# Taking 128 of 512 tokens out of a dense expert product and summing their gathered rows on VectorE

## What is computed

```
q = (hf @ w_q).reshape(T, 8, 2, 128)
s = einsum("thpd,hpkd->thpk", q, sub_keys)          # 128 keys per half
... top 16 per half, top 16 of their 256 sums per head
idx  = i1 * 128 + i2                                # 8 heads x 16 = 128 experts per token, of 16384
gate = softmax(best_v)
a    = einsum("tmd,td->tm", u_tab[idx], x)          # up: one dot product per picked expert
wgt  = gate * gelu(a)
y    = einsum("tm,tmd->td", wgt, v_tab[idx])        # down: weighted sum of the picked value rows
```

## Time and profile before

| | |
|---|---|
| median of 3 runs | 3601.62 us (3600.2 to 3602.76) |
| profiled execution, its own time | 3602.71 us |
| its span, first to last instruction | 3600.7 us |
| TensorE, VectorE, ScalarE, GpSimd busy | 97%, 67%, 29%, 12% |
| up stage of layer 0, gate chunks | about 605 to 1022 us |
| down stage, layer 0 | about 1109 to 1815 us |
| DMA traffic | 633.62 MB, mean 176 GB/s |

### The profile page before, as it was taken

How to read it: one execution, slowest core, us unless ns; L and a number is a source line. 1 busy time by engine, 2 the same in 40 slices (tenths; PEclk the granted TensorE clock), 3 DMA queues, 4 the chain that set the end, 5 groups by cost and what they waited for, 6 DMA issues and landing times.

```text
span 3600.7 us, 56122 instructions
## 1 busy us (share of the span) xinstructions
PE 3503.5 (97%) x16668; PEld 2836.9 (79%) x16668; DVE 2422.0 (67%) x6622; ACT 1039.3 (29%) x1382; POOL 438.8 (12%) x186
## 2 busy tenths in 40 slices
PE   5999999999999999999999999999999999999998
PEld 3578888888887888888875788888888888888886
DVE  6973996999924666665577159969999055555555
ACT  3333223444432212121242332234444312121122
POOL 0033443000031000000001334410000400000000
PEclk8999999999999999999999999999999999999999
DMA  6152443555547777786621224435555566666663
GB/s 221 58 215 90 146 143 138 186 199 216 216 181 222 243 235 243 243 244 195 181 93 37 78 97 143 146 132 216 216 181 204 204 204 193 193 192 195 190 196 119
DMA packets 442868, 633.62 MB, mean 176 GB/s; under 512 B 285984, under 2 KB 286368, under 8 KB 440352
## 3 DMA queue, kind: packets, MB, share of 16 engines
q1 hardware_dynamic: 402752, 495.60, 43.5%
q10 hardware_dynamic: 40032, 137.07, 9.7%
HBM read 496.26 MB, written 136.31 MB: 176 GB/s over the span
## 4 chain that ended last, share of the span: by engine, by line
PE 78%; DVE 16%; issue 3%; DMA 1%; ACT 1%; DVEq 0%; SPq 0%; ACTq 0%
PE bank L563 26%; PE bank L439 22%; PE bank L567 13%; PE bank L443 11%; PE bank L546 3%; DVE z_pad L1095 2%; DVE h L1060 2%; DVE h L1063 2%; DVE h L1062 1%; DVE h L1059 1%; DVE scratch L969 1%; DVE z_pad L1093 1%; DVE h L1096 1%; DVE u_pad L1061 1%; PE bank L362 1%
## 5 line engine op out<-in xcount | busy, mean ns | idle before, releaser
L598 ACT ACTIVATE w_hi<-ring 128x1024 fp32r<-128x1024 f32 x584 | 618.9, 1060 | 2243.0 <-PE bank L567 1110.7
L439 PE MATMUL bank<-h_hi,w_hi 128*128 128x512 f32 x2528 | 1000.3, 396 | 5.1 <-ACT scratch L598 2.3
L439 PE MATMUL bank<-h_lo,w_hi 128*128 128x512 f32 x2528 | 985.8, 390 | 0.0
L563 PE MATMUL bank<-v_hi,w_hi 128*128 128x512 f32 x2032 | 792.1, 390 | 5.7 <-DVE v_lo L1146 5.7
L563 PE MATMUL bank<-v_lo,w_hi 128*128 128x512 f32 x2032 | 791.8, 390 | 0.0
L782 POOL TENSOR_TENSOR w_lo<-ring,w_hi 128x1024 fp32r<-128x1024 f32 x172 | 437.1, 2543 | 1717.1 <-ACT w_hi L598 1717.1
L443 PE MATMUL bank<-h_hi,w_lo 128*128 128x512 f32 x2528 | 624.2, 389 | 0.0
L439 PEld LDWEIGHTS bank<-h_hi,w_hi 128*128 128x128 f32 x2528 | 474.8, 188 | 105.1 <-ACT w_hi L598 4.9
L443 PEld LDWEIGHTS bank<-h_hi,w_lo 128*128 128x128 f32 x2528 | 474.5, 188 | 98.5
L439 PEld LDWEIGHTS bank<-h_lo,w_hi 128*128 128x128 f32 x2528 | 474.9, 188 | 97.2 <-issue 1.4
L1131 DVE TENSOR_SCALAR h<-iota_b,keys 128x128 f16<-128x128 f16 x2048 | 543.5, 308 | 0.0
(11 more groups left out here) (147 smaller groups left out, 1990.9 us busy)
## 6 DMA issues: line engine op xcount, KB each, us to landing
ring<-u_t SPq DMA_DIRECT2D x256, 512.0 KB, 3.3
ring<-v_t SPq DMA_DIRECT2D x256, 512.0 KB, 3.4
ga_scratch<-norm_tmp ACTq DMA_DIRECT2D x256, 256.0 KB, 2.0
g_scratch<-scratch ACTq DMA_DIRECT2D x16, 4096.0 KB, 13.4
scratch<-ga_scratch SPq DMA_DIRECT2D x256, 256.0 KB, 3.8
scratch<-g_scratch SPq DMA_DIRECT2D x256, 256.0 KB, 4.2
scratch<-ada_t SPq DMA_DIRECT2D x76, 512.0 KB, 5.3
ring<-wq_t SPq DMA_DIRECT2D x32, 512.0 KB, 3.4
```

The source lines that it names most:

```text
L439: pe.matmul(to, w_hi[:, b, k * P:(k + 1) * P], part_h[:, k, :], start=(k == 0 and part_h is h_hi), stop=False)
L563: pe.matmul(bank[:, k, :], w_hi[:, b, k * P:(k + 1) * P], part_w[:, b, :], start=(first and part_w is v_hi), stop=False)
L598: return act.activation(to, of, ACT.Copy)
```

## The change

The last 128 tokens (`OWN` = 128) leave the gate matrix and the down product, which keep `TD` = 384 tokens. Those 128 tokens have 128 picks each. For each pick number there is one gather of a value row per token (128 rows of 4 KB), and VectorE adds it, times its weight, to `own_y` (tokens on the partitions). Their up product stays dense. The GELU values that belong to their picks are gathered from `ga_dram` one value at a time, 128 gathers of 128 values.

The parts of the diff that matter:

```
+    OWN = 128
+    TD = T - OWN
+    PICKS = HEADS * TOPK
+    TURNS = PICKS // PER_ROW
+    ROWS = 3
+    TOK = 8
+    EARLY, LATE = RETRIEVING + 2 * RING, TD // TOK
+    ADDS = 2 * ROWS
+    ADD_FIRST = 10
+    ADD_LAST = ADD_FIRST + TURNS // ADDS
+    ADA_AT = 1
```

SyncE, `load_back`: gates by pairs of chunks, 384 tokens; four chunks are loaded ahead, not three:

```
+                    if n % 2:
+                        pair = n // 2 % 2
+                        sp.dma_start(g_in[:, pair, :, :], g_dram[:, :, bass.ds(RING * first + (n - 1), 2), :]
+                                     .rearrange("b p c t -> p b (c t)")).then_inc(g_landed[pair], 16)
+                    sp.dma_start(ga_in[:, slot, :], ga_dram[c][:, 0:TD]).then_inc(ga_landed[slot], 16)
-                for n in range(RING - 1):
+                for n in range(RING):
                     load_back(0, n)
```

TensorE:

```
-                            pe.matmul(bank[:, k, :], w_hi[:, b, k * P:(k + 1) * P], part_w[:, b, :],
+                            pe.matmul(bank[:, k, 0:TD], w_hi[:, b, k * P:(k + 1) * P], part_w[:, b, 0:TD],
...
+                pe.wait_ge(own_done, l + 1)
...
+                    pe.matmul(bank[:, k, TD:T], own_y[:, k * P:(k + 1) * P], fold[:, :], start=True, stop=True)\
+                      .then_inc(down_done, 1)
```

ScalarE:

```
+                act.wait_ge(own_ready, l + 1)
+                for half in range(PER_ROW):
+                    for own, of in zip((own_i, own_e, own_g), picked):
+                        act.dma_start(own[half * OWN:(half + 1) * OWN, :], of[P - OWN:P, half * TURNS:(half + 1) * TURNS])\
+                           .then_inc(own_spread, 16)
...
+                def split_v(r, n):
+                    b = n % 2
+                    act.wait_ge(w_step, N_V * l + RING * r + (n + 1))
+                    wait_product(act, l, r, stages["v"] + n - 2)
+                    copy(v_hi[:, b, 0:TD], ga_in[:, n % RING, :]).then_inc(v_high, 1)
```

GpSimd (the low halves of the last up chunks go to VectorE):

```
+                pool.wait_ge(own_spread, 48 * PER_ROW * (l + 1))
+                def fetch_rows(n):
+                    pool.wait_ge(rows_used, TURNS * l + n + 1)
+                    pool.indirect_dma_start(own_rows[n % ROWS], None, v_rows,
+                                            bass.IndirectOffsetOnAxis(ap=own_i[:, n:n + 1].bitcast(U32), axis=0))\
+                        .then_inc(rows_landed[n % ROWS], 16)
+                for n in range(ROWS):
+                    fetch_rows(n)
+                for s in range(RING):
+                    pool.wait_ge(ga_stored[s], 16 * (N_U // RING) * l + 16 * (N_U // RING) + 16)
+                for n in range(TURNS):
+                    pool.indirect_dma_start(own_w[:, n:n + 1], None, ga_cells,
+                                            bass.IndirectOffsetOnAxis(ap=own_e[:, n:n + 1].bitcast(U32), axis=0))\
+                        .then_inc(cells_landed, 16)
+                for n in range(ROWS, TURNS):
+                    fetch_rows(n)
```

VectorE:

```
+                def add(n, i):
+                    s = i % ROWS
+                    dve.wait_ge(rows_landed[s], 16 * (TURNS // ROWS + (s < TURNS % ROWS)) * l + 16 * (ADDS // ROWS) * n
+                                + (16 * (i // ROWS) + 16))
+                    dve.wait_ge(rows_used, TURNS * l + ADDS * n + (ROWS + i))
+                    dve.scalar_tensor_tensor(own_y, own_rows[s], own_w[:, bass.ds(ADDS * n + i, 1)], own_y,
+                                             ALU.mult, ALU.add).then_inc(rows_used, 1)
...
+                def step(r, s, with_ada, own, last=False):
+                    low_halves(r, s)
+                    if not last:
+                        weights(r, s + 1)
+                    if own:
+                        own(r, s)
+                    if with_ada and s < ADA_STEP:
+                        wait_ada(dve, ada_landed, 16, l, s, r - ADA_AT)
+                        modulate(s, ADA_STEP * (r - ADA_AT) + s)
...
+                def late_add(r, s):
+                    for i in range(ADDS * s // RING, ADDS * (s + 1) // RING):
+                        add(r - ADD_FIRST, i)
+                def some_rounds(with_ada):
+                    rounds(ADA_AT, ADD_FIRST, with_ada, None)
+                    dve.wait_ge(cells_landed, 16 * TURNS * l + 16 * TURNS)
+                    dve.tensor_tensor(own_w, own_w, own_g, ALU.mult).then_inc(own_weighed, 1)
+                    dve.wait_ge(own_weighed, 2 * l + 2)
+                    settle(dve)
+                    rounds(ADD_FIRST, ADA_AT + ADA_ROUNDS, with_ada, late_add)
```

More of the change, by code:

```diff
@@ L117, in hybrid_encoder @@
         coef = sb("coef", [P, 2, KC])
+        fold = ident
+        row_base = sb("row_base", [P, 1])
+        own_token = sb("own_token", [P, 1])
         def part(at, n):
@@ L1150, in weights @@
                        .then_inc(tile_used[s], 1)
-                def rounds(start, end, with_ada):
+                def step(r, s, with_ada, own, last=False):
[7 more added lines that the diff above has]
+                        modulate(s, ADA_STEP * (r - ADA_AT) + s)
@@ L1153, in rounds @@
+                def rounds(start, end, with_ada, own):
                     with dve.Fori(start, end) as r:
                         for s in range(RING):
-                            weights(r, s)
-                            if with_ada and s < ADA_STEP:
-                                wait_ada(dve, ada_landed, 16, l, s, r)
-                                modulate(s, ADA_STEP * r + s)
+                            step(r, s, with_ada, own)
+                def late_add(r, s):
+                    for i in range(ADDS * s // RING, ADDS * (s + 1) // RING):
+                        add(r - ADD_FIRST, i)
@@ new lines, in some_rounds @@
+                def some_rounds(with_ada):
[5 more added lines that the diff above has]
+                    rounds(ADD_FIRST, ADA_AT + ADA_ROUNDS, with_ada, late_add)
+                weights(0, 0)
+                rounds(0, ADA_AT, False, None)
@@ L1160, in _ @@
                 with dve.If(l < LAST):
-                    rounds(0, ADA_ROUNDS, True)
+                    some_rounds(True)
                 with dve.Else():
-                    rounds(0, ADA_ROUNDS, False)
-                rounds(ADA_ROUNDS, N_V // RING, False)
+                    some_rounds(False)
+                rounds(ADA_AT + ADA_ROUNDS, ADD_LAST, False, late_add)
+                for i in range(REST):
+                    add(TURNS // ADDS + 0 * l, i)
+                dve.wait_ge(rows_used, TURNS * l + TURNS + ROWS)
@@ L1165, in _ @@
+                dve.nop().then_inc(own_done, 1)
+                assert ADD_LAST == N_V // RING - 1
+                for s in range(RING):
+                    step(N_V // RING - 1, s, False, None, s == RING - 1)
                 for k in range(KC):
```

164 lines of the change are left out of this document (102 added, 62 removed).

## The result

The changed kernel takes 3714.2 us (median of 4 runs, 3710.0 to 3719.3), the kernel before 3602.2 on the same chip: ratio 1.0317, with a 95% interval of 1.0304 to 1.033. It is 3.2% slower, where 3416 us and 5% faster were forecast. 298 us are missing, and they lie in one place.

The account below looks back on a forecast made before the run. TensorE, busy 97% of the span, was taken to bound the kernel. 3602.7 -327.7 (down product) -32.2 (gate stage) -2.9 (seam) +3.8 (folds) +166 (transfers) +8 (cells) -1.1 (median) gave 3416 us, range 3310 to 3560.

Parts of the forecast that it names:

- the cells: Down stage before round 10: 128 gathers of single values a layer end slightly late, +4 us a layer, +8 us.
- Down product, 173.3 ns: Down product: 384 columns instead of 512 make each matmul 173.3 ns and a chunk 4.16 us, 327.7 us less.
- Rival (d): Down product: weight loads bind at 188 ns, +32 us, 3448 us in all; chance 0.08, counted inside the main 0.52.
- Gate stage: Up product: 48 chunks instead of 64 carry gates, 32.2 us less over 2 layers.
- seam: Between up and down product: 8.1 us go, 2.6 us without cover are new, twice; net 2.9 us less.
- folds: End of the down stage: eight fold products of 128 columns in full f32 a layer, +3.8 us.
- VectorE: Down stage: VectorE alone would add 21 us in 15 of layer 0's rounds; no separate term in the sum.
- Transfers in the rounds with adds: Down stage, rounds 10 to 30: transfers stretch chunks to 5.6 and 4.9 us, +104 and +62, together +166 us.
- the prediction's lower bound of 4.4 us: Rounds 10 to 30: a chunk's transfers without modulation take 4.4 us at full rate, over the 4.16 us beat.
- A gather costs GpSimd 1.3 us: Down stage: each of the 128 cell gathers a layer was taken to cost GpSimd 1.3 us.
- Rival (c): Cells in the down stage: gathers above 2.02 us make the kernel slower than before; 3724 us at 2.5; chance 0.13.
- Nothing added for the port: Down stage: VectorE's two-input operations beside GpSimd's gathers were taken not to slow down, so 0 us added.

Follow-up runs that it names:

- e11: The changed kernel without the gathers of cells and value rows and without the 256 adds on VectorE; 3249.5 us.
- e3: The changed kernel with all 128 gathers of 4-byte pieces reading the same 128 neighbouring values; 3448.3 us.
- e12: The changed kernel with a wait before each cell gather for a value that is long reached, so nothing is paced; 3667.9 us.
- e14: The changed kernel with the first cell gather waiting until the down product has come to chunk 10; 3687.2 us.
- v2: The changed kernel, whole computation, 4-byte gathers paced at 2.7 a chunk, the last 32 behind row fetches, weighed in two parts; 3425.9 us.
- e16: As e10, but cell gather n waits for chunk n*39/128; 3493.3 us.
- e10: The changed kernel with cell gather n waiting until the down product has come to chunk n*40/128; 3447.0 us.
- e9: The changed kernel with the 128 cell gathers replaced by plain GpSimd copies of 4-byte pieces 256 KB apart; 3399.6 us.
- e7: The changed kernel with indexed 4-byte gathers where partition p always reads the first value of chunk p, 256 KB from the next; 3711.9 us.
- v1: The changed kernel, whole computation, gathering pieces of 256 bytes from which VectorE takes the own token's value with a mask; 3428.8 us.
- e15: The changed kernel with the cell gathers in bursts of 16, each waiting until the one before has landed; 3570.7 us.
- e13: The changed kernel with one small GpSimd write before each of the 128 cell gathers; 3659.6 us.
- e4: The changed kernel with the cell gathers replaced by 128 plain GpSimd copies of 4-byte pieces out of one chunk, 2 KB apart; 3401.7 us.

## Why the prediction was wrong

The step that failed is the last term of the sum, "the cells": "+4 us a layer, +8". It asked what 128 gathers cost GpSimd and whether they would be done in time. It didn't ask what they do to TensorE while they run.

1. *Down product, 173.3 ns.* Right: 1101.21 to 1101.38, and 24 of them from 1101.21 to 1105.37, 4.16 us. Rival (d) is out; the loads follow at the same distance though each is written with 188 ns.
2. *Gate stage, seam, folds, VectorE.* Right in sum: e11 has none of the terms behind them and takes 3249.5 for 3243. The seam itself was forecast too short. TensorE waits 3.59 us there (3.58 in layer 1) and not 2.6, and the stretch at the 1.2 GHz level is still there, with starts 0.32 us apart from 1096.71 to 1099.59, some 1.5 us lost, where nothing was put down for it. Together that is 2.5 us a layer, most of the 6.5:

```profile
1095.37 0.44 PE L594 MATMUL bank<-v_hi,w_hi 128*128 128x384 f32 x1 [3.59 <-DVE v_lo L1259]
...
1096.71 0.53 PE L594 MATMUL bank<-v_lo,w_hi 128*128 128x384 f32 x1
1097.03 0.53 PE L594 MATMUL bank<-v_hi,w_hi 128*128 128x384 f32 x1
```

3. *Transfers in the rounds with adds.* Right in sum, by errors that cancel. The windows from the first start of chunk 40 to that of chunk 124, which are rounds 10 to 30 of each layer:

```profile
1422.50:1886.11 463.61, 385.92 (x2017) 372.07 (x2017) 366.69 (x439) 124.20 (x168) 147.09 (x125) 0.93 0.95 341
3287.89:3672.45 384.56, 362.64 (x2017) 351.33 (x2016) 333.18 (x379) 124.25 (x168) 132.10 (x125) 0.99 1.02 370
```

In layer 0 this is 463.6 / 84 = 5.52 us a chunk, where the forecast is (60 x 5.6 + 24 x 4.9) / 84 = 5.4; in layer 1 it is 384.6 / 84 = 4.58 instead of 4.9. The cost was 10 us too low in layer 0 and 27 us too high in layer 1. The share is 0.95 and 1.02, so the engines bind and not the three buffers, and layer 1 comes near the prediction's lower bound of 4.4 us. By the runs, rows and adds cost 154 us instead of 166. The mean of 370 GB/s over 385 us, like the 387 in a slice of the page, is over the limit of about 358 that the prediction cited from the Trainium skill (DMA: Bandwidth & Descriptors, section Specifications).
4. *A gather costs GpSimd 1.3 us.* Right for the changed kernel (1.30 in the mean), but only because VectorE stood still there for most of the time. Beside a working VectorE it is 1.48 us (1.41 in layer 1), and even without the fall the cells would cost 45 us (e3), not 8.
5. *The rest, some 265 us,* is TensorE's fall to one instruction in 1.4 us. It was in no rival, and the forecast put it at nothing without naming it. Rival (c) had a time close to it (3724) for a reason that the trace refutes: it asked for gathers above 2.02 us, VectorE waiting for cells, and a gap before round 10. They take 1.30, and the gaps are between TensorE's own instructions. That the two times are close is luck.
6. *Nothing added for the port.* Right for VectorE, whose operations stay at 1.22 us beside the gathers; GpSimd bore it.

What makes TensorE fall stays open. The runs show what it takes (indexed gathers of pieces of 4 or 64 bytes, spread wide) and what it is not: the tensor, the 4 bytes alone, the distance alone, the number of gathers, or a load on the DMA engines. They also show that the ends of its instructions are late before the starts are. That a slow TensorE must be able to slow the gathers for a cure is what e12 to e14 against v2 and e16 speak for; e10, which never visibly paused before 1261 us and didn't fall, isn't explained by it. Between e9 and e7 the GpSimd queue moves the same 4096 packets for the 128 transfers, but e9's are issued at twice the rate, and the order of the pieces over the DMA engines may differ; I had no run that separates this from the indices. Each execution here also has a recorded span and clock, so no run shows whether the recording of TensorE's instructions has a part in it. Pieces of 128 bytes and pitches between 2 and 256 KB weren't tried with indices.

Of the kernels that compute the whole, the fastest are v2 with 3425.9 us and v1 with 3428.8 (they can't be told apart, as their runs overlap). e10 and e16 also beat both kernels, by less, and e15 the one before by 0.8%. v1 and v2 are 8% faster than the changed kernel and 4.9% and 4.7% faster than the one before.

## What to carry to other kernels

Price a gather three times: what its engine needs to issue it beside the others that work then (here 1.25 us alone, 1.48 beside a busy VectorE), what the bytes cost, and whether the engine that sets the end keeps its beat while it runs; only a trace tells the third. Fetch 256 bytes and pick the value on VectorE rather than gather single values from all over HBM; where they must be single, tie them to the progress of the main loop so that it can recover. If a busy engine shows equal gaps put down to "issue", with no wait and idle transfers, look at what starts and ends with them on other engines before looking at its own code, and at how late the others learn that its work is done.

## What was unexpected of the hardware

- Beside indexed gathers of 128 scattered pieces of 4 or 64 bytes, TensorE took 1.4 us for each instruction, a load of 128x128 or a matmul of 384 columns alike, where a pair takes 0.173 us otherwise. The ends were told up to 88 us after the starts. Pieces of 256 bytes, 4-byte pieces side by side, and plain copies 256 KB apart didn't do it.
- In layer 0 it sets in some 15 to 70 us after the first gather and lasts, unpaced, to the end of the gathers (but for e13 in layer 1 and e15's pauses). The gathers themselves are quicker meanwhile (1.25 us instead of 1.48).
- The instruction queues carry next to nothing meanwhile. The changed kernel's transfers between 1095 and 1275 us, with packets, MB and share:

```profile
q8 instruction: 1, 0.02, 0.0%
q14 instruction: 1, 0.01, 0.0%
```

- Plain GpSimd copies of 128 pieces followed each other every 0.57 us and could be hidden whole (e4, e9); an indexed gather kept GpSimd for 0.94 to 2.0 us, with 0.30 to the next.
